# Opening of a two-layer decoder trunk: another order of the first loads and transposes, and a shorter run of warm-up matmuls

## The chip, the cores and the metric

The kernel runs on one core of a Trainium2 chip. The metric is the device time of one execution in microseconds (us), the median over several runs. The profile is one further execution on the same kind of chip.

## The reference

Two layers over 272 tokens (16 learned meta tokens in front of 256 tokens of x), model width 1024, float32. What matters here is the start: the first sub-layer norms the rows and multiplies them by the first weight matrix.

```python
h = jnp.concatenate([meta, x], axis=1)
for l in range(DEPTH):
    g = norm_g[l]
    h = h + 0.5 * rmsnorm(swiglu(rmsnorm(h, g[FFN1_PRE]), ffn_w_in[l, 0], ffn_w_out[l, 0]), g[FFN1_POST])
    ...   # pooling mixer, windowed attention, gated merge, second SwiGLU
return h[:, N_META:]
```

## The kernel before

Activations are kept transposed: `h` and `x_hi`/`x_lo` are eight tiles of 128 model columns by 272 tokens. Every float32 product is made of three matmuls on TensorE (function `products`, lines 451 to 453), with weights and activations split into a high and a low part: weights high by activations high, weights high by activations low, weights low by activations high. A "unit" is 256 output columns of a weight matrix (1024 KB, tile `raw`). SP loads units one after another into a ring of four slots; ScalarE makes `w_hi` from `raw`, VectorE makes `w_lo = raw - w_hi`. A whole unit is 2 x 8 x 3 = 48 matmuls of 272 columns.

The opening is written out by hand, in the order in which each engine's program lists it:

- **SP** (lines 344 to 356) loads the first half of x's columns, the second half, then the first half of unit 0 (line 366), its second half (line 356) and the further units. Each of the two halves of x and of unit 0 is 512 KB. The second half of x has a semaphore of its own, `second_half_in`.
- **ScalarE's queue** (lines 1037 to 1040) loads `norm_g` as 96 rows of 128 (the norms' rows), the meta tokens, and `pool_scale` as 8 more rows. These three and x's first half count on the one semaphore `inputs_in`.
- **TensorE** (lines 832 to 845) waits for the identity matrix, runs `WARM_FIRST` = 3 matmuls of the identity by itself, 512 columns each, whose result nobody reads, waits for all four transfers of `inputs_in`, transposes the 104 rows of norm gains and pool scales (`small`, bank 7), and then for each of the eight column blocks k transposes meta, first and second 128 tokens of x into bank k: a trio (lines 843, 844, 845). Ahead of k = 4 it waits for x's second half; ahead of k = 7 it waits until the rows in bank 7 have been read. Each trio raises `first_T`.
- **VectorE** copies the rows out (`g_all`, line 1501; `g_next`, the gains of the first norm, line 1503), and then, alternating with ScalarE, copies the trios into `h` (`first_h`, lines 1508 and 1047). ScalarE scales `h` into `x_hi` (line 1055), VectorE makes `x_lo` (line 1252), and between these unit 0 is split in four pieces of two column blocks each (`first_split`, line 1065 on ScalarE, line 1518 on VectorE).
- **TensorE** then runs the products of units 0 and 1 (`first_pair`): 12 matmuls for each piece of unit 0, each piece behind its own semaphore.

Of the kernel before, what the change touches and what calls it, by code (L numbers as in the profile page):

```python
# [33 lines left out]
P = 128  # L34
# [4 lines left out]
DEPTH = 2  # L39
# [9 lines left out]
KD = D // P  # L49
KF = FF // P  # L50
UW = 2 * P
# [35 lines left out]
NORMS = 6  # L87
# [56 lines left out]
def trunk(nc, x, meta_tokens, norm_g, ffn_w_in, ffn_w_out, w_in, pool_w_grp, pool_scale, w_pool_proj,  # L144
          sinks, w_attn_proj, w_o, geometry, out):
    with ExitStack() as ctx:
# [3 lines left out]
        def sem(name):  # L150
            return ctx.enter_context(nc.semaphore(name))


        raw = sb("raw", [P, RING, KD * UW])
# [21 lines left out]
        ident = sb("ident", [P, P])  # L176
        ones = sb("ones", [P, 1])
        g_all = sb("g_all", [P, DEPTH * NORMS * KD + DEPTH * GROUPS])
        g_cur = sb("g_cur", [P, NORMS * KD])
        half_g = sb("half_g", [P, KD])  # L180
        g_next = sb("g_next", [P, KD])
# [51 lines left out]
        n_rows = DEPTH * NORMS * KD + DEPTH * GROUPS  # L233
        first_rows = gates[0:n_rows, 12, 0:P]
# [6 lines left out]
        pT_bank, pTm_bank, o_bank, small = bank[4], bank[5], bank[6], bank[7]  # L241
        warm = o_bank
        S_SUM, S_BC = 0, 128


        inputs_in = sem("inputs_in")
        second_half_in = sem("second_half_in")
        geo_in = sem("geo_in")
        raw_landed = [sem(f"raw_landed{s}") for s in range(RING)]
# [8 lines left out]
        layer_consts = sem("layer_consts")  # L258
        first_T = sem("first_T")
        first_odd = sem("first_odd")  # L260
        first_raw = sem("first_raw")
# [3 lines left out]
        rows_read = sem("rows_read")  # L265
# [75 lines left out]
        @block.sync  # L341
        def _(sp):

            sp.dma_start(first_x[:, :, 0:D // 2], x[0, :, 0:D // 2].rearrange("(b p) d -> p b d", b=2)
                         ).then_inc(inputs_in, 16)
            sp.dma_start(first_x[:, :, D // 2:D], x[0, :, D // 2:D].rearrange("(b p) d -> p b d", b=2)
                         ).then_inc(second_half_in, 16)

# [4 lines left out]
            def load(u, src, dst=None):  # L353
                s = u % RING
                to = raw[:, s, 0:unit_k(u) * UW].rearrange("p (k c) -> p k c", c=UW) if dst is None else dst
                sp.dma_start(to, src).then_inc(raw_landed[s], 16)

            def ffn_loads(l, f):
                w1 = ffn_w_in[ds(l, 1), f].rearrange("o (k p) n -> p (o k) n", p=P)
                w2 = ffn_w_out[ds(l, 1), f].rearrange("o (k p) n -> p (o k) n", p=P)  # L360
                u0 = U_FFN_IN[f]
                for j in range(2):
                    slot_free(u0 + j, l)
                    if l == 0 and u0 + j == 0:
                        to = raw[:, 0, :].rearrange("p (k c) -> p k c", c=UW)
                        sp.dma_start(to[:, 0:KD // 2, :], w1[:, 0:KD // 2, 0:UW]).then_inc(first_raw, 16)
                        load(0, w1[:, KD // 2:KD, 0:UW], to[:, KD // 2:KD, :])
                    else:
                        load(u0 + j, w1[:, :, j * FF:j * FF + UW])
                with sp.Fori(0, N_IN - 5, 4) as i:  # L370
                    for j in range(4):
                        slot_free(u0 + 2 + j, l, i)
                        load(u0 + 2 + j, w1[:, :, ds(i * (UW // 2) + (UW * (1 + j // 2) + j % 2 * FF), UW)])
                u0 = U_FFN_OUT[f]
                if token_major(l, f):
                    for n in range(2):
                        for g, (k, nk) in enumerate(zip(END_K0, END_K)):
                            u = u0 + 6 * n + g
                            slot_free(u, l)
                            load(u, w2[:, k:k + nk, n * HALF_D:(n + 1) * HALF_D],  # L380
                                 raw[:, u % RING, 0:nk * HALF_D].rearrange("p (k c) -> p k c", c=HALF_D))
                    slot_free(u0 + N_END, l)
                    load(u0 + N_END, norm_g[l, NORMS - 1:NORMS, :].to_broadcast([P, D]), raw[:, (u0 + N_END) % RING, 0:D])
                    return
                with sp.Fori(0, N_OUT - 3, 4) as i:
                    for j in range(4):
                        slot_free(u0 + j, l, i)
                        load(u0 + j, w2[:, OUT_K0[j]:OUT_K0[j] + OUT_K[j], ds(i * (UW // 4), UW)])

            for l in range(DEPTH):  # L390
# [4 lines left out]
                for u in range(U_K, U_PP):  # L395
# [6 lines left out]
                    if U_Q <= u < U_POOL:  # L402

                        c = q0 + (8 * ((u - U_Q) // 2) + 2 * ((u - U_Q) % 2)) * DH
# [35 lines left out]
        def _(pe):  # L440
# [391 lines left out]
            pe.wait_ge(consts, 1)  # L832
            for _ in range(WARM_FIRST):
                pe.matmul(warm[:, :], ident[:, :], ident[:, :].unsqueeze(1).to_broadcast([P, 4, P]), start=True, stop=True)
            pe.wait_ge(inputs_in, 16 * 4)
            pe.transpose(small[:, 0:n_rows], first_rows, ident[0:n_rows, 0:n_rows]).then_inc(first_T, 1)
            for k in range(KD):
                if k == KD // 2:
                    pe.wait_ge(second_half_in, 16)
                if k == KD - 1:  # L840
                    pe.wait_ge(rows_read, 1)
                b = bank[k]
                pe.transpose(b[:, 0:META], first_meta[:, k * P:(k + 1) * P], ident[0:META, 0:META])
                pe.transpose(b[:, B1], first_x[:, 0, k * P:(k + 1) * P], ident[:, :])
                pe.transpose(b[:, B2], first_x[:, 1, k * P:(k + 1) * P], ident[:, :]).then_inc(first_T, 1)
# [15 lines left out]
        def _(act):  # L861
# [171 lines left out]
            def merge_hi(m, l):  # L1033
                act.wait_ge(merged, l * KD + m + 1)
                act.activation(x_hi[:, m, :], gates[:, m, :], ACT.Copy, scale=0.5).then_inc(xhi_ready, 1)

            act.dma_start(first_rows[0:DEPTH * NORMS * KD, :], norm_g.rearrange("l n (k p) -> (l n k) p", p=P)
                          ).then_inc(inputs_in, 16)
            act.dma_start(first_meta, meta_tokens).then_inc(inputs_in, 16)
            act.dma_start(first_rows[DEPTH * NORMS * KD:n_rows, :], pool_scale.rearrange("l (g p) -> (l g) p", p=P)  # L1040
                          ).then_inc(inputs_in, 16)
            act.preload_act_table(ACT.Silu)

            def first_h(k):

                act.wait_ge(first_T, k + 2)
                act.activation(h[:, k, :], bank[k][:, 0:T], ACT.Copy).then_inc(first_odd, 1)

            def first_operand(k):
# [19 lines left out]
            for piece in range(4):  # L1069
                k = 2 * piece  # L1070
# [12 lines left out]
            act.dma_start(sink_all[:, :], sinks.rearrange("(o l) h -> o (l h)", o=1).to_broadcast([P, DEPTH * HEADS])  # L1083
                          ).then_inc(geo_in, 16)
            split_hi(2, 0)
            act.wait_ge(inputs_in, 16 * 4)
            act.wait_ge(second_half_in, 16)
            scratch = y[:, :, :].rearrange("p k t -> p (k t)")
            for b, rows_of in enumerate((first_x[:, 0, :], first_x[:, 1, :], first_meta)):
# [75 lines left out]
        def _(dve):  # L1165
# [23 lines left out]

            def layer_columns(l):  # L1190
                dve.wait_ge(geo_in, 32)

                dve.wait_ge(xlo_ready, l * 4 * KD + KD)
                dve.wait_ge(h_ready, l * 3 * KD + KD)
                scales = DEPTH * NORMS * KD
                dve.tensor_copy(g_cur[:, :], g_all[:, ds(l * (NORMS * KD), NORMS * KD)])
                dve.tensor_copy(scale_cur[:, :], g_all[:, ds(l * GROUPS + scales, GROUPS)])
                for g in range(2):

                    dve.tensor_copy(sink_cur[:, 8 * g:8 * g + 8].rearrange("p (t s) -> p s t", s=2),  # L1200
                                           sink_all[:, ds(l * HEADS + 8 * g, 8)].rearrange("p (s t) -> p s t", s=2)
                                    ).then_inc(sinks_set, 1)

                dve.wait_ge(sinks_set, 2 * l + 2)
                dve.tensor_scalar(minus_sink[:, :], sink_cur[:, :], -1.0, None, ALU.mult)
                dve.tensor_scalar(half_g[:, :], g_all[:, ds(l * (NORMS * KD) + (NORMS - 1) * KD, KD)], 0.5, None, ALU.mult)

                dve.tensor_copy(g_next[:, :], g_all[:, ds(l * (NORMS * KD) + NORMS * KD, KD)]).then_inc(layer_consts, 1)
                dve.wait_ge(layer_consts, l + 2)
# [287 lines left out]
                                         ).then_inc(xlo_ready, 1)  # L1497


            dve.wait_ge(first_T, 1)  # L1500
            dve.tensor_copy(g_all[:, :], small[:, 0:n_rows]).then_inc(rows_read, 1)
            dve.wait_ge(rows_read, 1)
            dve.tensor_copy(g_next[:, :], g_all[:, 0:KD]).then_inc(layer_consts, 1)

            def first_h(k):

                dve.wait_ge(first_T, k + 2)
                dve.tensor_copy(h[:, k, :], bank[k][:, 0:T]).then_inc(h_ready, 2)

            def first_split(u, piece):  # L1510
# [8 lines left out]
                                  ).then_inc(lo_done if piece == pieces - 1 else first_lo, 1)  # L1519

            first_h(0)
            first_h(2)
            for piece in range(4):
                k = 2 * piece
                if piece == 0:
                    x_low(0, g_next, k)
                    first_split(0, 0)
                    x_low(0, g_next, k + 1)
                else:
                    x_low(0, g_next, k)  # L1530
                    x_low(0, g_next, k + 1)
                    first_split(0, piece)
                if piece < 2:
                    first_h(k + 4)
# [250 lines left out]
END_BANKS = ((4, 5), (0, 1))  # L1785
G_SLOT = (U_FFN_OUT[1] + N_END) % RING
Q_BANKS = ((4, 5), (0, 1), (2, 3), (0, 1))
WARM_FIRST = 3
WARM_RMS, WARM_X = 5, 5

META_STEP = 6
# [40 lines left out]
```

## Time and profile before

| | |
|---|---|
| Device time, median of 3 runs | 1208.03 us (1207.97 to 1208.48) |
| Device time of the profiled execution | 1207.88 us |
| Its span, first to last instruction | 1206.1 us |
| TensorE busy | 1193.3 us (99%) |
| VectorE, ScalarE, GpSimd busy | 708.4, 540.8, 448.4 us |
| Mean DMA rate | 164 GB/s |

The profile is of one execution. In the tables below PE is TensorE's matmul side and PEld its weight loads, DVE is VectorE, ACT ScalarE, POOL GpSimd, SP SyncE; a q behind a name (SPq, ACTq) is an engine's queue of issued transfers. A busy PE is not yet a PE at its peak, since matmuls are pipelined and their ends are modelled; it is the distance between starts that tells the pace. The device time of the profiled execution is 1.8 us longer than its span, for what lies around the instructions.

### The profile page before, as it was taken

The numbers are of one execution on the slowest core, as the hardware profiler recorded it, in microseconds if no ns is written. First come the engines' busy times: TensorE is split into PE (matmuls) and PEld (weight loads), VectorE is DVE, ScalarE is ACT, GpSimd is POOL, SyncE is SP. The second block draws the span as 40 slices with busy tenths as digits, with TensorE's granted clock in tenths as the row PEclk, the third lists the DMA queues.
The fourth block names the chain that finished last, engine by engine and source line by source line (L and its number), as shares of the span: only waits on it lengthen the run. The fifth ranks groups of instructions, "written<-read, shape, count | busy, mean of one in ns | idle before, by whom it ended". The sixth has DMA issues, their size and how long they took to land.

```text
span 1206.1 us, 23922 instructions
## 1 busy us (share of the span) xinstructions
PE 1193.3 (99%) x9352; PEld 1157.5 (96%) x9352; DVE 708.4 (59%) x1036; ACT 540.8 (45%) x763; POOL 448.4 (37%) x520
## 2 busy tenths in 40 slices
PE   9999999999999999999999999999999999999997
PEld 7999999999999999999999999999999999999986
DVE  6655544768666765544477554447776667755542
ACT  6433334536653453333344333344466545534441
POOL 0854500206312375542127554112064123865600
PEclk9999999999999999999999999999999999999999
DMA  9655357363355455535636553563734553655540
GB/s 315 201 174 165 123 184 226 102 210 108 100 134 189 136 176 174 174 122 172 215 120 198 181 171 117 185 200 110 226 124 106 166 185 105 210 189 176 180 169 35
DMA packets 197614, 197.59 MB, mean 164 GB/s; under 512 B 4136, under 2 KB 190736, under 8 KB 197536
## 3 DMA queue, kind: packets, MB, share of 16 engines
q1 hardware_dynamic: 197088, 196.10, 51.5%
q8 instruction: 56, 0.92, 0.3%
q10 hardware_dynamic: 448, 0.39, 0.1%
q14 instruction: 22, 0.18, 0.0%
HBM read 195.43 MB, written 1.05 MB: 163 GB/s over the span
## 4 chain that ended last, share of the span: by engine, by line
PE 93%; DVE 4%; issue 1%; POOL 1%; ACT 1%; DVEq 0%; POOLq 0%; ACTq 0%
PE bank L451 27%; PE bank L453 27%; PE bank L452 27%; PE bank L659 2%; PE bank L661 2%; PE bank L660 2%; DVE w_lo L1172 1%; PE bank L748 1%; PE bank L743 1%; PE bank L555 1%; DVE tmp L1261 1%; DVE h L1268 1%; PE bank L702 1%; DVE x_lo L1252 1%; PE bank L713 0%
## 5 line engine op out<-in xcount | busy, mean ns | idle before, releaser
L451 PE MATMUL bank<-x_hi,w_hi 128*128 128x272 f32 (+1 forms) x1988 | 575.0, 289 | 1.6 <-DVE up_r L1303 1.0
L453 PE MATMUL bank<-x_hi,w_lo 128*128 128x272 f32 (+1 forms) x1988 | 569.9, 287 | 0.0
L452 PE MATMUL bank<-x_lo,w_hi 128*128 128x272 f32 (+1 forms) x1988 | 568.3, 286 | 0.0
L870 ACT ACTIVATE w_hi<-raw 128x2048 fp32r<-128x2048 f32 (+2 forms) x210 | 352.6, 1686 | 436.6 <-PE bank L453 425.7
L1172 DVE TENSOR_TENSOR w_lo<-raw,w_hi 128x2048 fp32r<-128x2048 f32 (+3 forms) x208 | 423.8, 2045 | 164.4 <-ACT w_hi L870 159.3
L451 PEld LDWEIGHTS bank<-x_hi,w_hi 128*128 128x128 f32 x1988 | 374.6, 188 | 3.5 <-issue 1.5
L452 PEld LDWEIGHTS bank<-x_lo,w_hi 128*128 128x128 f32 x1988 | 374.4, 188 | 0.3
L453 PEld LDWEIGHTS bank<-x_hi,w_lo 128*128 128x128 f32 x1988 | 374.5, 188 | 0.0
L1718 POOL TENSOR_TENSOR hid_hi<-silu,up_r 128x272 f32 x88 | 140.4, 1595 | 177.1 <-DVE up_r L1303 157.1
L451 PE MATMUL bank<-hid_hi,w_hi 128*128 128x272 f32 x528 | 153.0, 290 | 0.0
L453 PE MATMUL bank<-hid_hi,w_lo 128*128 128x272 f32 x528 | 152.7, 289 | 0.0
L452 PE MATMUL bank<-hid_lo,w_hi 128*128 128x272 f32 x528 | 152.3, 288 | 0.0
L1303 DVE TENSOR_TENSOR up_r<-bank,r 128x272 f32<-128x272 f32 x88 | 38.4, 440 | 111.5 <-PE bank L453 103.7
L451 PEld LDWEIGHTS bank<-hid_hi,w_hi 128*128 128x128 f32 x528 | 99.6, 189 | 0.0
L452 PEld LDWEIGHTS bank<-hid_lo,w_hi 128*128 128x128 f32 x528 | 99.6, 189 | 0.0
L453 PEld LDWEIGHTS bank<-hid_hi,w_lo 128*128 128x128 f32 x528 | 99.3, 188 | 0.0
L1296 DVE TENSOR_TENSOR gate_r<-bank,r 128x272 f32<-128x272 f32 x88 | 38.0, 439 | 98.2 <-PE bank L453 98.1
L1723 POOL TENSOR_TENSOR hid_lo<-hid_f,hid_hi 128x272 f32 x88 | 87.9, 999 | 20.1 <-POOL hid_f L1720 20.1
L1702 POOL TENSOR_TENSOR acc<-acc,sq 128x272 f32<-128x272 f32 x50 | 41.8, 836 | 113.5 <-ACT sq L880 111.0
L1720 POOL TENSOR_TENSOR hid_f<-silu,up_r 128x272 f32<-128x272 f32 x88 | 77.6, 882 | 0.0
L1699 POOL TENSOR_TENSOR acc<-sq 128x272 f32<-128x272 f32 x10 | 11.7, 1166 | 153.5 <-ACT sq L880 153.5
L1754 POOL TENSOR_TENSOR acc<-s,stats 128x16 f32<-128x16 f32 x64 | 16.7, 261 | 89.5 <-DVE stats L1449 89.2
(204 smaller groups left out, 1277.9 us busy)
## 6 DMA issues: line engine op xcount, KB each, us to landing
raw<-in_ffn_w_in SPq DMA_DIRECT2D x87, 1024.0 KB, 5.1
raw<-in_w_in SPq DMA_DIRECT2D x24, 1024.0 KB, 5.6
raw<-in_ffn_w_out SPq DMA_DIRECT2D x24, 768.0 KB, 4.4
raw<-in_ffn_w_out SPq DMA_DIRECT2D x24, 640.0 KB, 4.0
raw<-in_ffn_w_out SPq DMA_DIRECT2D x10, 1024.0 KB, 5.1
raw<-in_w_in SPq DMA_DIRECT2D x16, 512.0 KB, 5.3
raw<-in_w_attn_proj SPq DMA_DIRECT2D x32, 256.0 KB, 4.2
raw<-in_w_o SPq DMA_DIRECT2D x8, 1024.0 KB, 5.4
```

The costliest lines, as they stand in the source:

```text
L451: pe.matmul(ps[:, t0:T], w[0], a_hi[:, t0:T], start=start, stop=False)
L452: pe.matmul(ps[:, t0:T], w[0], a_lo[:, t0:T], start=False, stop=False)
L453: return pe.matmul(ps[:, t0:T], w[1], a_hi[:, t0:T], start=False, stop=stop)
L659: pe.matmul(ps[:, :], hid_hi[:, k, cols], w[0], start=k == 0, stop=False)
L870: last = act.activation(hi, w, ACT.Copy)
L1172: last = dve.tensor_tensor(lo, w, hi.bitcast(F32), ALU.subtract)
L1296: dve.tensor_tensor(gate_r[:, j, :], bank[4 * (unit // 2 % 2) + j][:, 0:T], r[:, :], ALU.mult).then_inc(tile_read, 1)
L1303: dve.tensor_tensor(up_r[:, j, :], bank[2 + j][:, 0:T], r[:, :], ALU.mult).then_inc(tile_read, 1)
L1702: pool.tensor_tensor(acc[:, :], acc[:, :], sq[:, m % 2, :], ALU.add).then_inc(acc_done, 1)
L1718: pool.tensor_tensor(hid_hi[:, ds(i * 2 + j, 1), :].rearrange("p o t -> p (o t)"), silu[:, j, :], up_r[:, j, :], ALU.mult).then_inc(hid_hi ...
L1720: pool.tensor_tensor(hid_f[:, j, :], silu[:, j, :], up_r[:, j, :], ALU.mult).then_inc(hf_ready, 1)
L1723: pool.tensor_tensor(hid_lo[:, ds(i * 2 + j, 1), :].rearrange("p o t -> p (o t)"), hid_f[:, j, :], hid_hi[:, ds(i * 2 + j, 1), :].rearrang ...
```

## The change

SP now issues, in this order: the norms' rows (`norm_g`, which left ScalarE's queue), x's first half, the first half of unit 0, x's second half, the second half of unit 0. The norms' rows and the pool scales have a semaphore of their own (`rows_in`), so TensorE's first wait is for x's first half and the meta tokens alone. The transposed rows come ahead of k = 2 instead of ahead of k = 0. VectorE takes `g_next` straight from the bank between `first_h(0)` and `first_h(2)`, and `g_all` behind `first_h(2)`. The warm-up is one matmul of 512 columns and two of 256, for three of 512.

```diff
@@ block.sync
+            sp.dma_start(first_rows[0:DEPTH * NORMS * KD, :], norm_g.rearrange("l n (k p) -> (l n k) p", p=P)
+                         ).then_inc(rows_in, 16)
             sp.dma_start(first_x[:, :, 0:D // 2], x[0, :, 0:D // 2].rearrange("(b p) d -> p b d", b=2)
                          ).then_inc(inputs_in, 16)
+            first_w = ffn_w_in[0:1, 0].rearrange("o (k p) n -> p (o k) n", p=P)[:, :, 0:UW]
+            first_to = raw[:, 0, :].rearrange("p (k c) -> p k c", c=UW)
+            sp.dma_start(first_to[:, 0:KD // 2, :], first_w[:, 0:KD // 2, :]).then_inc(first_raw, 16)
             sp.dma_start(first_x[:, :, D // 2:D], x[0, :, D // 2:D].rearrange("(b p) d -> p b d", b=2)
                          ).then_inc(second_half_in, 16)
...
-                        to = raw[:, 0, :].rearrange("p (k c) -> p k c", c=UW)
-                        sp.dma_start(to[:, 0:KD // 2, :], w1[:, 0:KD // 2, 0:UW]).then_inc(first_raw, 16)
-                        load(0, w1[:, KD // 2:KD, 0:UW], to[:, KD // 2:KD, :])
+                        load(0, first_w[:, KD // 2:KD, :], first_to[:, KD // 2:KD, :])
@@ block.tensor
             for _ in range(WARM_FIRST):
                 pe.matmul(warm[:, :], ident[:, :], ident[:, :].unsqueeze(1).to_broadcast([P, 4, P]), start=True, stop=True)
-            pe.wait_ge(inputs_in, 16 * 4)
-            pe.transpose(small[:, 0:n_rows], first_rows, ident[0:n_rows, 0:n_rows]).then_inc(first_T, 1)
+            for _ in range(WARM_SHORT):
+                pe.matmul(warm[:, 0:2 * P], ident[:, :], ident[:, :].unsqueeze(1).to_broadcast([P, 2, P]), start=True, stop=True)
+            pe.wait_ge(inputs_in, 16 * 2)
             for k in range(KD):
+                if k == 2:
+                    pe.wait_ge(rows_in, 16 * 2)
+                    pe.transpose(small[:, 0:n_rows], first_rows, ident[0:n_rows, 0:n_rows]).then_inc(first_T, 1)
@@ block.scalar
-            act.dma_start(first_rows[0:DEPTH * NORMS * KD, :], norm_g.rearrange("l n (k p) -> (l n k) p", p=P)
-                          ).then_inc(inputs_in, 16)
...
             def first_h(k):
-                act.wait_ge(first_T, k + 2)
+                act.wait_ge(first_T, k + 1 if k < 2 else k + 2)
@@ block.vector
-            dve.wait_ge(first_T, 1)
-            dve.tensor_copy(g_all[:, :], small[:, 0:n_rows]).then_inc(rows_read, 1)
-            dve.wait_ge(rows_read, 1)
-            dve.tensor_copy(g_next[:, :], g_all[:, 0:KD]).then_inc(layer_consts, 1)
...
             first_h(0)
+            dve.wait_ge(first_T, 3)
+            dve.tensor_copy(g_next[:, :], small[:, 0:KD]).then_inc(layer_consts, 1)
             first_h(2)
+            dve.tensor_copy(g_all[:, :], small[:, 0:n_rows]).then_inc(rows_read, 1)
+            dve.wait_ge(layer_consts, 1)
...
-WARM_FIRST = 3
+WARM_FIRST, WARM_SHORT = 1, 2
```

SP's transfers at the start of the program, before:

```order
L344 DMA gates<-in_x 128x2x512
L346 DMA gates<-in_x 128x2x512
L366 DMA raw<-in_ffn_w_in 128x4x256 [waits lo_done]
L356 DMA raw<-in_ffn_w_in 128x4x256
L356 DMA raw<-in_ffn_w_in 128x8x256 [waits lo_done]
```

and with the change:

```order
L345 DMA gates<-in_norm_g 96x128
L347 DMA gates<-in_x 128x2x512
L351 DMA raw<-in_ffn_w_in 128x4x256
L352 DMA gates<-in_x 128x2x512
L362 DMA raw<-in_ffn_w_in 128x4x256 [waits lo_done]
L362 DMA raw<-in_ffn_w_in 128x8x256 [waits lo_done]
```

x's second half, second in SP's queue before, is now the fourth transfer and the third of 512 KB; `norm_g` stands ahead of all.

TensorE from the warm-up to the fifth trio (k = 4), before; the 128x104 row is the transpose of the norms' rows, a 128x16 row opens a trio:

```order
L834 MATMUL bank<-ident 128x512 [waits consts]
L834 MATMUL bank<-ident 128x512 x2
L836 MATMUL bank<-ident,gates 128x104 [waits inputs_in]
L843 MATMUL bank<-ident,gates 128x16
L844 MATMUL bank<-ident,gates 128x128
L845 MATMUL bank<-ident,gates 128x128
...
L843 MATMUL bank<-ident,gates 128x16 [waits second_half_in]
```

and with the change:

```order
L838 MATMUL bank<-ident 128x512 [waits consts]
L840 MATMUL bank<-ident 128x256 x2
L851 MATMUL bank<-ident,gates 128x16 [waits inputs_in]
L852 MATMUL bank<-ident,gates 128x128
L853 MATMUL bank<-ident,gates 128x128
...
L845 MATMUL bank<-ident,gates 128x104 [waits rows_in]
...
L851 MATMUL bank<-ident,gates 128x16 [waits second_half_in]
```

Two trios now stand ahead of the rows' transpose; the waits ahead of the fifth trio and of the eighth are where they were.

VectorE's first instructions, before:

```order
L1501 COPY g_all<-bank 128x104 [waits first_T]
L1503 COPY g_next<-g_all 128x8 [waits rows_read]
L1508 COPY h<-bank 128x272 [waits first_T] x2
L1252 SCALAR_TENSOR_TENSOR x_lo<-h,g_next,x_hi 128x272 [waits xhi_ready]
L1518 TENSOR_TENSOR w_lo<-raw,w_hi 128x512 [waits first_hi]
```

and with the change:

```order
L1510 COPY h<-bank 128x272 [waits first_T]
L1525 COPY g_next<-bank 128x8 [waits first_T]
L1510 COPY h<-bank 128x272 [waits first_T]
L1527 COPY g_all<-bank 128x104
L1259 SCALAR_TENSOR_TENSOR x_lo<-h,g_next,x_hi 128x272 [waits xhi_ready,layer_consts]
L1520 TENSOR_TENSOR w_lo<-raw,w_hi 128x512 [waits first_hi]
```

The copy `g_all` moved from the front to just ahead of the first `x_lo`.

## Rows read from the trace of the kernel before

**Rows 1.** Windows: us, PE busy (x), PEclk, DMA share, GB/s.
```profile
30.00:1200.00 1170.00, 1165.03 (x9178) 1.00 0.51 160
```

**Rows 2.** Chain of waits, opening: start us, us, what.
```profile
1.35 0.30 POOL ident L1691
1.70 5.45 PE bank L834 x6
7.15 0.26 PE bank L836
7.41 0.16 PE bank L843
...
11.28 0.26 PE bank L844
11.90 0.13 PE bank L453
```

**Rows 3.** Timeline, weight loads of TensorE: start us, us, what [idle before].
```profile
2.71 0.34 PEld L834 LDWEIGHTS bank<-ident 128*128 128x128 f32 x1 [0.52 <-issue]
...
4.42 0.34 PEld L834 LDWEIGHTS bank<-ident 128*128 128x128 f32 x1 [0.52 <-issue]
5.27 0.34 PEld L834 LDWEIGHTS bank<-ident 128*128 128x128 f32 x1 [0.52 <-issue]
7.10 0.14 PEld L836 LDWEIGHTS bank<-ident,gates 104*128 104x128 f32 x1 [1.49 <-DMA gates<-in_pool_scale]
```

**Rows 4.** Timeline, SP's issues of transfers.
```profile
0.75 0.45 SPq L344 DMA_DIRECT2D gates<-in_x  x1
1.27 0.45 SPq L346 DMA_DIRECT2D gates<-in_x  x1
1.77 0.46 SPq L366 DMA_DIRECT2D raw<-in_ffn_w_in  x1
```

**Rows 5.** Lines 346 and 366: from issue to landing.
```profile
L346 SPq DMA_DIRECT2D gates<-in_x x1: 445/445/445, 1.3 to 1.3; - x1
...
DMA to landing us min/median/max: 5.9/5.9/5.9
...
L366 SPq DMA_DIRECT2D raw<-in_ffn_w_in x1: 460/460/460, 1.8 to 1.8; - x1
...
DMA to landing us min/median/max: 6.9/6.9/6.9
```

**Rows 6.** Timeline, TensorE: fifth trio (k = 4), last transpose, first product.
```profile
9.46 0.23 PE L843 MATMUL bank<-ident,gates 16*128 16x16 f32 x1
...
9.99 0.23 PE L843 MATMUL bank<-ident,gates 16*128 16x16 f32 x1
...
11.40 0.37 PE L451 MATMUL bank<-x_hi,w_hi 128*128 128x272 f32 x1
```

**Rows 7.** Timeline, ScalarE and VectorE in the opening.
```profile
8.50 0.40 ACT L1047 ACTIVATE h<-bank 128x272 f32<-128x272 f32 x1 [4.82 <-PE bank L845]
8.80 0.51 ACT L1055 ACTIVATE x_hi<-h,g_next 128x272 fp32r<-128x272 f32 x1
...
7.45 0.27 DVE L1501 COPY g_all<-bank 128x104 f32<-128x104 f32 x1 [7.45 <-PE bank L836]
7.75 0.17 DVE L1503 COPY g_next<-g_all 128x8 f32<-128x8 f32 x1
...
9.46 0.49 DVE L1252 SCALAR_TENSOR_TENSOR x_lo<-h,g_next,x_hi 128x272 fp32r<-128x272 f32 x1
...
13.83 0.69 DVE L1518 TENSOR_TENSOR w_lo<-raw,w_hi 128x512 fp32r<-128x512 f32 x1
...
24.06 2.29 DVE L1172 TENSOR_TENSOR w_lo<-raw,w_hi 128x2048 fp32r<-128x2048 f32 x1 [1.52 <-ACT w_hi L870]
```

**Rows 8.** Timeline, weight loads around the third piece of unit 0.
```profile
14.12 0.19 PEld L452 LDWEIGHTS bank<-x_lo,w_hi 128*128 128x128 f32 x1
14.24 0.19 PEld L453 LDWEIGHTS bank<-x_hi,w_lo 128*128 128x128 f32 x1
14.57 0.19 PEld L451 LDWEIGHTS bank<-x_hi,w_hi 128*128 128x128 f32 x1
```

**Rows 9.** Weight loads of the identity, lines 834 and 565: ns min/median/max, first and last start us.
```profile
L834 PEld LDWEIGHTS bank<-ident x6: 287/337/337, 1.7 to 5.3; 128*128 128x128 f32 x6
...
L565 PEld LDWEIGHTS bank<-ident x60: 190/192/192, 214.4 to 824.8; 128*128 128x128 f32 x60
```

More of the change, by code:

```diff
@@ L246, in trunk @@
         inputs_in = sem("inputs_in")
+        rows_in = sem("rows_in")
         second_half_in = sem("second_half_in")
@@ L1035, in merge_hi @@
                 act.activation(x_hi[:, m, :], gates[:, m, :], ACT.Copy, scale=0.5).then_inc(xhi_ready, 1)
-            act.dma_start(first_rows[0:DEPTH * NORMS * KD, :], norm_g.rearrange("l n (k p) -> (l n k) p", p=P)
-                          ).then_inc(inputs_in, 16)
             act.dma_start(first_meta, meta_tokens).then_inc(inputs_in, 16)
             act.dma_start(first_rows[DEPTH * NORMS * KD:n_rows, :], pool_scale.rearrange("l (g p) -> (l g) p", p=P)
-                          ).then_inc(inputs_in, 16)
+                          ).then_inc(rows_in, 16)
             act.preload_act_table(ACT.Silu)
             def first_h(k):
-                act.wait_ge(first_T, k + 2)
+                act.wait_ge(first_T, k + 1 if k < 2 else k + 2)
                 act.activation(h[:, k, :], bank[k][:, 0:T], ACT.Copy).then_inc(first_odd, 1)
@@ L1085, in _ @@
             split_hi(2, 0)
-            act.wait_ge(inputs_in, 16 * 4)
+            act.wait_ge(inputs_in, 16 * 2)
             act.wait_ge(second_half_in, 16)
@@ L1191, in layer_columns @@
                 dve.wait_ge(geo_in, 32)
+                dve.wait_ge(rows_read, 1)
                 dve.wait_ge(xlo_ready, l * 4 * KD + KD)
@@ L1497, in merge_lo @@
                                          ).then_inc(xlo_ready, 1)
-            dve.wait_ge(first_T, 1)
-            dve.tensor_copy(g_all[:, :], small[:, 0:n_rows]).then_inc(rows_read, 1)
-            dve.wait_ge(rows_read, 1)
-            dve.tensor_copy(g_next[:, :], g_all[:, 0:KD]).then_inc(layer_consts, 1)
             def first_h(k):
-                dve.wait_ge(first_T, k + 2)
+                dve.wait_ge(first_T, k + 1 if k < 2 else k + 2)
                 dve.tensor_copy(h[:, k, :], bank[k][:, 0:T]).then_inc(h_ready, 2)
```

## The prediction

> **What bounds the kernel now.** I read the windows first, then the chain of waits, then the timeline of the opening engine by engine. From 30 to 1200 us TensorE is busy for 1165.0 of 1170 us [rows 1]. Behind the opening the kernel is one stream of matmuls, so a change of the opening is worth what it moves the start of that stream, unless something behind it is tied to absolute time. The chain of waits shows what sets that start [rows 2]: GpSimd makes the identity, TensorE runs the warm-up from 1.70 to 7.15, then the rows' transpose and the trios without a gap, and the first products follow. The first product starts at 11.40 [rows 6]. One gap remains in the first unit: weight loads follow each other by 0.12 or 0.13 us, except 14.24 to 14.57 [rows 8], a stall of 0.20, because the third piece of `w_lo` is ready only at 13.83 + 0.69 = 14.52 [rows 7].
>
> **Why the first transpose starts at 7.10.** The warm-up loads are 0.85 us apart (4.42 to 5.27), one for each pass of 512 columns, two passes to a float32 matmul [rows 3]. The first pass therefore starts at 2.71 - 0.85 = 1.86 and the six end at 1.86 + 6 x 0.85 = 6.97. The load for the rows' transpose starts at 7.10; the trace names the `pool_scale` transfer as what it waited for [rows 3]. So warm-up and inputs end within 0.13 us of each other and I can't tell which is last. Removing warm-up alone may then be worth nothing. The change does both: it shortens the warm-up and asks for fewer transfers first.
>
> **The change, part by part.**
>
> Warm-up: one matmul of 512 columns and two of 256 make 2 x 0.85 + 4 x 0.43 = 3.4 us, so it ends at 5.27 in place of 6.97: 1.7 us removed.
>
> First trio: it needs x's first half and meta. The trace has no landing for the first half. The second of SP's 512 KB transfers landed at 1.27 + 5.9 = 7.17 and the third at 1.77 + 6.9 = 8.67 [rows 4, 5], 1.50 apart; one step back gives 5.7 (an estimate). The issue now stands one place later, 0.52 us by the distance of SP's issues [rows 4], so 5.7 to 6.2. I take 6.2. Four trios at 9.99 - 9.46 = 0.53 [rows 6] and the rows' transpose at 0.26 [rows 2] make 2.4 us: k = 3 is done at 8.6.
>
> Fifth trio, the term that decides: it needs x's second half, before the second 512 KB of SP's queue and now the third. What was third landed at 8.67, and the same bytes stand ahead of it in both orders (`norm_g`, meta, `pool_scale`, two transfers of 512 KB). The ends: 8.67 if nothing is lost at the start, 9.2 if the whole queue slips by the 0.52 of one issue more. Less than that slips, as the small `norm_g` gives the engines something to move meanwhile: I take 8.80. With 0.05 from semaphore to start (the identity is done at 1.65, TensorE starts at 1.70 [rows 2]) the fifth trio starts at 8.85, and k = 3 is done by then. From fifth trio to first product took 11.40 - 9.46 = 1.94 [rows 6]. First product: 8.85 + 1.94 = 10.79, that is **0.61 earlier**. Moving x's second half back thus eats most of the 1.7 us of warm-up: TensorE waits there instead.
>
> The splits: ScalarE's chain was started by the second trio (`first_h(1)` at 8.50, `x_hi` at 8.80 [rows 7]). Now the second trio ends at 6.2 + 1.06 = 7.3, the rows are transposed by 7.5, `g_next` (0.17 [rows 7]) is there at 7.75, and the first half of unit 0, now second in the queue, has landed at 7.17 to 7.7. So ScalarE starts `x_hi` about 1.0 earlier. VectorE must take h for k = 2 (third trio done 8.1) and then the moved `g_all` (0.27 [rows 7]) ahead of the first `x_lo`: 8.1 + 0.4 + 0.3 = 8.8 against 9.46, 0.66 earlier. Between that `x_lo` and the third piece's end at 14.52 the timeline has no idle time of VectorE, so the third piece is ready at about 13.86. TensorE gets there at 10.79 + (14.37 - 11.40) = 13.76. Of the stall of 0.20 about 0.10 stays and **0.10 to 0.15 goes**.
>
> `g_all` behind `first_h(2)`: the eighth trio waits until bank 7 is read. That is at about 8.8, and the trio comes at 8.85 + 3 x 0.53 = 10.4. Cost nothing; a `g_all` 1.6 us later would begin to cost. One DMA moved from ScalarE's queue to SP's: ScalarE had nothing to do until 8.50 [rows 7], so nothing; its price on SP is the slip above. The wait for `rows_in`: `norm_g` is first of all and `pool_scale` second on ScalarE's queue, both small. They land ahead of the 7.3 at which TensorE asks. If `pool_scale` came with x's second half, ScalarE's chain would start at 9 and the gain would be gone.
>
> Later loads: the second half of unit 0 keeps its place as the fourth 512 KB. The `w_lo` of unit 3 is done at 24.06 + 2.29 = 26.35 [rows 7], while TensorE needs it three units of 48 x 0.125 = 6.0 us after 11.4, at 29.4: 3 us of slack, so an earlier stream doesn't run into its weights.
>
> Sum: 0.61 + 0.14 = 0.75 us less. For the profiled execution 1207.88 - 0.75 = 1207.1; the median of the runs stands 0.15 above it, so **1207.3 us**. A measurement of this kernel tells about 0.2% from no change, that is 2.4 us; the whole warm-up removed is less than that.
>
> **A rival on the other side: the clock rises later.** The granted clock reads 1.00 in every window, but the weight loads of the identity took 0.337 us in the warm-up and 0.192 from 214 us on, in the same form [rows 9], and the load at 7.10 took 0.14 [rows 3]. I read this as the lower level (1.2 GHz) up to about 7 us and the upper (2.4 GHz) from there, the warm-up having kept TensorE busy for 5.1 us before. The change gives it 3.4 us, a gap until x lands, then transposes with a gap before k = 4. The traces show that transposes behind the rise stayed quick; none shows a rise during transposes. If it does not come, the transposes cost between nothing and double. In the middle, times 1.5, the first four trios and the rows end at 6.2 + 3.6 = 9.8, the last four at 9.8 + 2.9 = 12.7. The 1.7 us of missing matmuls are then made up by products at half rate, which costs 0.85: 13.55 against 11.40, less the stall of 0.20, is 1.95 us more: **1210.0**. At the ends: if the transposes cost no more, 10.79 + 0.85 against 11.40, less 0.20, is +0.04; with all of them doubled and 5.1 us of products at half rate 6.2 + 4.8 + 3.9 + 2.55 = 17.45 less 11.40 and 0.20, +5.85. It decides when the clock is still low at 8.85. Against it: TensorE's work is nearly as dense as before up to 8 us. Chance 0.22.
>
> The Trainium skill (TensorE: Matmul & The Clock Gate, Part 4) says that the full clock doesn't engage for transpose-mode matmuls. By that rule the shorter warm-up is a loss, since from 5.3 us on only transposes could raise the clock; the rival above is what it would do here. The trace neither shows nor excludes it.
>
> **Rival: the queue slips whole.** x's second half lands at 9.2: the fifth trio starts 0.4 later, first product 11.19, and the chain of splits is then not late: 0.21 + 0.20 less, **1207.6**. For it: SP's issues are evenly spaced; against it: the bytes ahead are the same. Chance 0.13.
>
> **Rival: x lands sooner.** If the first half is there at 5.7 and the second at 8.1, the transposes run without a gap: first product 5.7 + 8 x 0.53 + 0.26 = 10.2, 1.2 earlier, and the stall goes too: **1206.6**. It needs the early transfers faster than any row shows. Chance 0.12.
>
> **How the numbers follow.** Forecast 1207.3 with 0.48, its own range 1207.0 to 1207.6; 0.05 stay for something not thought of. The range goes down to 1206.4 (x sooner) and up to 1209.8, which leaves out the worse half of the clock's rival and the unknown: some 0.15. Slower by over 0.2% (above 1210.4) only comes from that rival's upper end: 0.07. Faster by over 0.2% (below 1205.6) would need more than the whole warm-up: 0.01. Within 0.2%: 0.92.
>
> **What would show it.** In the profile after: warm-up loads ending near 4.9; the first trio at 5.5 to 6.2; a gap of TensorE ahead of the fifth trio, named as the transfer of x, until about 8.85; the first product at 10.8; the distance at the third piece 0.13 to 0.25; weight loads of the transposes 0.14 us long. Loads of 0.34 in the transposes, or products more than 0.13 apart behind the first, would show the clock's rival. No gap ahead of k = 4 would show that x lands sooner. The forecast is wrong if the first product starts before 10.3 or after 11.4, or if the move of the first product is not found in the total.

## The result, and the profile after

The changed kernel takes 1211.09 us (median of 21 runs, 1207.42 to 1211.70); the kernel before, run beside it, 1208.07 (21 runs). The medians are 3.02 us apart, 0.25%; the ratio of the two is 1.0019, 95% interval 1.0013 to 1.0025. **Slower, where 0.75 us less was forecast**, and above the range (1206.4 to 1209.8).

| | before | after |
|---|---|---|
| Device time of the profiled execution | 1207.88 us | 1211.70 us |
| Span | 1206.1 us | 1209.9 us |
| TensorE busy | 1193.3 us | 1196.2 us |
| First trio starts | 7.34 us | 6.57 us |
| First product starts [rows 6] | 11.40 us | 13.13 us |

The stream behind the opening is as dense as before [rows 1]: of 1170 us TensorE is busy for 1165.3 (window: us, PE busy, PEclk, DMA share, GB/s).

```profile
30.00:1200.00 1170.00, 1165.28 (x9187) 1.00 0.51 160
```

So the loss lies in the opening, or in a clock that this column of busy time does not see. TensorE in the timeline of the changed kernel (start us, us, engine, line, operation): the end of the warm-up, the first two trios, the fifth, the last transpose and the first products.

```profile
3.56 1.91 PE L840 MATMUL bank<-ident 128*128 128x256 f32 x4
6.57 0.28 PE L851 MATMUL bank<-ident,gates 16*128 16x16 f32 x1 [1.09 <-DMA gates<-in_x]
...
7.40 0.28 PE L851 MATMUL bank<-ident,gates 16*128 16x16 f32 x1
...
9.72 0.42 PE L853 MATMUL bank<-ident,gates 128*128 128x128 f32 x1
10.08 0.28 PE L851 MATMUL bank<-ident,gates 16*128 16x16 f32 x1
...
13.06 0.42 PE L853 MATMUL bank<-ident,gates 128*128 128x128 f32 x1
13.13 0.58 PE L455 MATMUL bank<-x_hi,w_hi 128*128 128x272 f32 x1
...
13.73 0.43 PE L457 MATMUL bank<-x_hi,w_lo 128*128 128x272 f32 x1
13.96 0.43 PE L455 MATMUL bank<-x_hi,w_hi 128*128 128x272 f32 x1
```

The trios are 0.83 us apart (6.57, 7.40) against 0.53 before [rows 6], the products 0.23 apart against 0.125. The weight loads show where that ends:

```profile
16.23 0.33 PEld L457 LDWEIGHTS bank<-x_hi,w_lo 128*128 128x128 f32 x1
16.45 0.33 PEld L455 LDWEIGHTS bank<-x_hi,w_hi 128*128 128x128 f32 x1
16.68 0.22 PEld L456 LDWEIGHTS bank<-x_lo,w_hi 128*128 128x128 f32 x1
16.84 0.19 PEld L457 LDWEIGHTS bank<-x_hi,w_lo 128*128 128x128 f32 x1
16.97 0.19 PEld L455 LDWEIGHTS bank<-x_hi,w_hi 128*128 128x128 f32 x1
```

Up to 16.7 us a load takes 0.33 us and the loads are 0.23 apart, from there 0.19 and 0.125. I read this as TensorE at its lower clock (1.2 GHz) through the whole opening and 3.6 us into the products, where before it was at the upper one (2.4 GHz) from about 7 us. The granted clock column does not help for this stretch: it reads 1.00 wherever the trace holds no earlier entry.

**The account.** First product later: 13.13 - 11.40 = 1.73. From 13.13 to 16.7 some sixteen products start 0.227 apart in place of 0.125: 1.6 more. The stall at the third piece of `w_lo` [rows 8] is gone, 0.2 less, as slow products give the splits time. Together 3.1; matched matmul by matmul, the two traces stand 3.12 apart from 30 to 300 us. Two steps follow, 0.35 at 618 us and 0.36 at 1008. Sum 3.83; the spans differ by 3.8. The second step is a dip of the clock:

```profile
1005.00:1010.00 5.00, 4.51 (x37) 1.00 0.16 40
1010.00:1013.40 3.40, 3.40 (x17) 0.50 1.07 369
1013.40:1200.00 186.60, 185.89 (x1333) 1.00 0.47 153
```

(Windows: us, PE busy, PEclk, DMA share, GB/s.) It falls at the norm ahead of the last feed-forward, where TensorE waits. This step goes with the execution and not with the change: e10 and e15 below are one kernel, and the clock dips in the one and not in the other (the same columns):

```profile
1005.75:1009.10 3.35, 3.35 (x18) 0.50 1.08 370
1005.75:1009.10 3.35, 2.98 (x24) 1.00 0.99 338
```

So of the 3.8 us between the two profiles 3.5 belong to the change. The chain of waits of the opening begins with SP's first transfer, then x's:

```profile
0.75 0.40 SPq L345
1.22 5.31 DMA gates<-in_x
6.57 0.28 PE bank L851
6.85 0.41 PE bank L852
```

Before, it began with the identity and the warm-up [rows 2]. The landings that answer to [rows 5], of x's first half (issued at 1.22) and its second half (issued at 2.19):

```profile
L347 SPq DMA_DIRECT2D gates<-in_x x1: 412/412/412, 1.2 to 1.2; - x1
...
DMA to landing us min/median/max: 5.3/5.3/5.3
...
L352 SPq DMA_DIRECT2D gates<-in_x x1: 507/507/507, 2.2 to 2.2; - x1
...
DMA to landing us min/median/max: 7.3/7.3/7.3
```

The first half was there at 6.5, the second at 9.5, both later than forecast (6.2 and 8.8). The second cost nothing here: the slow trios brought TensorE to the fifth only at 10.08, and the gap that the prediction puts ahead of it is not there.

### The profile page after: what moved, and what is told of

Same layout as the page of the kernel before. It is cut to its first block, busy times and chain, and to the rows that moved or that the text cites. A ratio compares the mean times of both kernels' runs of the same rounds, so it can differ in the third digit from the quotient of the medians.

```text
span 1209.9 us, 23925 instructions
## 1 busy us (share of the span) xinstructions
PE 1196.2 (99%) x9352; PEld 1161.5 (96%) x9352; DVE 708.0 (59%) x1036; ACT 541.0 (45%) x763; POOL 448.4 (37%) x520
## 4 chain that ended last, share of the span: by engine, by line
PE 94%; DVE 3%; issue 1%; POOL 0%; DMA 0%; ACT 0%; DVEq 0%; SPq 0%; POOLq 0%
PE bank L455 27%; PE bank L457 27%; PE bank L456 27%; PE bank L663 2%; PE bank L665 2%; PE bank L664 2%; PE bank L559 1%; PE bank L752 1%; PE bank L747 1%; DVE w_lo L1178 1%; DVE tmp L1268 1%; DVE h L1275 1%; PE bank L706 1%; DVE x_lo L1259 1%; PE bank L717 0%
## 5 line engine op out<-in xcount | busy, mean ns | idle before, releaser
L1760 POOL TENSOR_TENSOR acc<-s,stats 128x16 f32<-128x16 f32 x64 | 16.7, 261 | 89.5 <-DVE stats L1456 89.1
```

## The experiments

Each was timed beside the kernel before on the same chip. "Late" counts runs at 1210 us or above.

**e2, the short warm-up alone.**

```diff
 (kernel before)
-WARM_FIRST = 3
+WARM_FIRST, WARM_SHORT = 1, 2
...
+            for _ in range(WARM_SHORT):
+                pe.matmul(warm[:, 0:2 * P], ident[:, :], ident[:, :].unsqueeze(1).to_broadcast([P, 2, P]), start=True, stop=True)
```

> The kernel before with nothing but the short warm-up (one of 512, two of 256 columns). Theory clock: trios of 0.83 us and products 0.227 apart at first, 2 to 4 us slower in most runs. Theory loads: the loads are those of before, so no more than 0.3 us from before. A third outcome: the inputs land at 6.6, the trios then fill the time and the clock comes up some 3.4 us later, so 1 to 2 us slower.

Measured 1211.89 against 1208.50, ratio 1.0023 (1.0014 to 1.0032), 11 of 11 late. Its loads:

```profile
17.07 0.32 PEld L452 LDWEIGHTS bank<-x_lo,w_hi 128*128 128x128 f32 x1
17.30 0.21 PEld L453 LDWEIGHTS bank<-x_hi,w_lo 128*128 128x128 f32 x1
17.45 0.19 PEld L451 LDWEIGHTS bank<-x_hi,w_hi 128*128 128x128 f32 x1
```

The clock rose at 17.3, 3.1 us behind the first product (14.20), with all transfers in their old order. The warm-up alone makes the loss.

**e1, the change with the warm-up of before.**

```diff
 (changed kernel)
-WARM_FIRST, WARM_SHORT = 1, 2
+WARM_FIRST, WARM_SHORT = 3, 0
```

> The changed kernel with the warm-up of before (three matmuls of 512 columns). Theory clock: the loss of 3 us is the short warm-up; with the long one the granted clock is up by about 7 us as in the kernel before, the transposes take 0.53 us a trio, and the first product starts when x's second half has landed (9.48 in the changed kernel's trace) plus 0.05 and 1.94, at 11.5: within 0.3 us of the kernel before. Theory loads: the loss is the late landing of x (6.5 and 9.5), so the time stays about 3 us above before.

Measured 1208.44 against 1208.50, ratio 0.9995 (0.9986 to 1.0004), none of 11 late. The loss is gone.

```profile
6.63 0.23 PE L851 MATMUL bank<-ident,gates 16*128 16x16 f32 x1
...
7.16 0.23 PE L851 MATMUL bank<-ident,gates 16*128 16x16 f32 x1
...
10.78 0.37 PE L455 MATMUL bank<-x_hi,w_hi 128*128 128x272 f32 x1
```

Trios 0.53 apart, first product at 10.78, 0.62 earlier than before. x's second half landed at 8.7 here, the first in time for 6.63. The full warm-up took 5.00 us in this execution against 5.45 [rows 2], since the clock rose inside it; the start of the trios gains by that too, and it is not the work of the change. Behind the first unit the stream is 0.47 ahead of before; a step of 0.35 at 618 us and one of 0.37 at 1008 (the clock dips there in this execution too) take it back.

**e3, the norms' rows ahead of x, nothing else.**

```diff
 (kernel before; removed from ScalarE's queue, and ahead of x on SP's)
+            sp.dma_start(first_rows[0:DEPTH * NORMS * KD, :], norm_g.rearrange("l n (k p) -> (l n k) p", p=P)
+                         ).then_inc(inputs_in, 16)
```

> The kernel before with only the norms' rows moved to the head of SP's queue, all waits and the warm-up as before. If it is that transfer that made x's first half land at 6.5, it does so here (the rows' transpose then starts at 7.1 or later) and the first product moves by 0 to 0.5 us; if the mixing of the queues makes it, the landing of x's second half stays at 7.2 and nothing moves. Theory clock: 0 to 0.5 us, far from 3.

Measured 1207.88 against 1208.50, ratio 0.9987 (0.9978 to 0.9997); ten of 11 between 1207.42 and 1208.19, one at 1438.83. The four inputs were in by 6.4, not 7.1, and the first product started at 10.70. In the profile the gain was lost at once (span 1206.1, as before), because the first half of unit 0, third of the 512 KB transfers, landed at 9.3 and ScalarE waited for it:

```profile
8.07 0.51 ACT L1055 ACTIVATE x_hi<-h,g_next 128x272 fp32r<-128x272 f32 x1
9.29 0.63 ACT L1065 ACTIVATE w_hi<-raw 128x512 fp32r<-128x512 f32 x1 [0.70 <-DMA raw<-in_ffn_w_in]
```

and TensorE behind it, 0.64 and 0.22 ahead of the second and the third piece:

```profile
12.89 0.19 PEld L453 LDWEIGHTS bank<-x_hi,w_hi 128*128 128x128 f32 x1 [0.64 <-DVE w_lo L1518]
...
14.66 0.19 PEld L453 LDWEIGHTS bank<-x_hi,w_hi 128*128 128x128 f32 x1 [0.22 <-DVE w_lo L1518]
```

The median is lower than the profile explains. Part of that is that none of the ten was late, where 9 of the 33 runs beside it were: the others of those have their median at 1208.25, 0.4 above e3's.

**e4, e1 with x's second half ahead of the first half of unit 0.**

```diff
 (e1; block.sync)
-            sp.dma_start(first_to[:, 0:KD // 2, :], first_w[:, 0:KD // 2, :]).then_inc(first_raw, 16)
             sp.dma_start(first_x[:, :, D // 2:D], x[0, :, D // 2:D].rearrange("(b p) d -> p b d", b=2)
                          ).then_inc(second_half_in, 16)
+            sp.dma_start(first_to[:, 0:KD // 2, :], first_w[:, 0:KD // 2, :]).then_inc(first_raw, 16)
```

> The changed kernel with the warm-up of before and x's second half ahead of the first half of unit 0. Theory clock: the clock is up by 7 us, no gap ahead of k = 4; the rows' transpose no longer stands ahead of the first trio, so the second trio ends 0.25 us earlier, the first product starts at 7.10 + 0.25 + 8 x 0.53 = 11.35 or so: between 0 and 0.3 us faster than before. Theory loads: the same as e1 less what the second half waited, so slower than before as long as the rows stand ahead of x.

Measured 1208.34, ratio 0.9995 (0.9986 to 1.0004), none of 11 late. First product at 10.72, then the same waits as in e3 (ScalarE 0.69, TensorE 0.58 and 0.22): behind the first unit it is level with before. e1, with weights ahead of x, is 0.47 ahead there, without the long waits. That the new order of transfers is worth this half microsecond is not shown: the medians of e1 and e4 are 1208.44 and 1208.34, and e10 and e15, both with the new order, are 0.63 and 0.10 ahead at the same place.

**e8, e1 with the norms' rows back at the head of ScalarE's queue.**

```diff
 (e1)
-            sp.dma_start(first_rows[0:DEPTH * NORMS * KD, :], norm_g.rearrange("l n (k p) -> (l n k) p", p=P)
+            act.dma_start(first_rows[0:DEPTH * NORMS * KD, :], norm_g.rearrange("l n (k p) -> (l n k) p", p=P)
```

> e1 (the change's order, warm-up of before) with the norms' rows back at the head of ScalarE's queue, so that x's first half is first on SP's. If the rows ahead of x delay it, x's first half lands about 0.5 us earlier than in e1 and the second half at 8.2 to 8.7; the first product then starts at 10.3 to 10.7 and the time is 0 to 0.5 us below e1. If the warm-up's end sets the first trio, nothing changes against e1.

Measured 1208.33 against 1208.53, ratio 0.9994 (0.9986 to 1.0003), none of 12 late. x's second half landed at 9.2, not 8.7, and the stream was level with before. The landings of one order differ by half a microsecond and more between executions (8.7, 9.0 and 8.9 in e1, e10, e15; 9.5 in the changed kernel), so one profile each does not settle which queue is better. Inconclusive.

**e7, a warm-up of 4.3 us** (as e2, with two matmuls of 512 columns and one of 256).

```diff
 (kernel before)
-WARM_FIRST = 3
+WARM_FIRST, WARM_SHORT = 2, 1
```

> The kernel before with a warm-up of two matmuls of 512 columns and one of 256, 4.3 us in all, between the 3.4 of e2 and the 5.1 of before. If whether the clock rises depends on where the start of the program falls, this length should give both outcomes: some runs near 1208, some 3 us above, the median in either place. If there is a sharp length, all runs are alike.

Measured 1211.49, ratio 1.0017 (1.0008 to 1.0025), 12 of 12 late: as bad as 3.4 us. The clock rose at 17.7.

**e5 and e6, what the warm-up is made of.**

```diff
 (kernel before; e5, with WARM_FIRST = 20)
-                pe.matmul(warm[:, :], ident[:, :], ident[:, :].unsqueeze(1).to_broadcast([P, 4, P]), start=True, stop=True)
+                pe.transpose(warm[:, 0:P], ident[:, :], ident[:, :])
 (e6, with WARM_FIRST = 12)
+                pe.matmul(warm[:, 0:P], ident[:, :], ident[:, :], start=True, stop=True)
```

> The kernel before with its warm-up made of 20 transposes of the identity (128 columns each, 0.26 us apart at the lower clock, 5.2 us in all) in place of three matmuls of 512 columns (5.1 us). Theory kind (transposes do not bring the clock up): the clock rises only 3 to 4 us after the first product, as in e2, and the time is 3 to 4 us above before. Theory length (any 5 us of TensorE work do): as before, within 0.3 us.

> The counterpart: 12 plain matmuls of the identity, 128 columns each, about 5.1 us in all. Both theories: the clock rises by 7 us and the time is that of before within 0.3 us. If this too is 3 us slower, it is the width of the matmuls and not their kind.

e6: 1208.93, ratio 1.0002 (0.9992 to 1.0011), 3 of 10 late. Narrow matmuls do as well as wide ones. e5: 1211.43, ratio 1.0017 (1.0008 to 1.0027), 10 of 10 late. The time seems to speak for "kind", but e5 does not have the length that was meant: its transposes started 0.21 us apart, not 0.26, so twenty of them make 4.3 us in place of 5.1, as short as e7's warm-up, and e7 was late in all runs with plain matmuls. The time doesn't separate kind from length. The trace speaks against "kind":

```profile
1.70 4.53 PE L834 MATMUL bank<-ident 128*128 128x128 f32 x20 [1.70 <-POOL ident L1691]
...
8.72 0.23 PE L843 MATMUL bank<-ident,gates 16*128 16x16 f32 x1
...
9.25 0.23 PE L843 MATMUL bank<-ident,gates 16*128 16x16 f32 x1
...
10.50 0.28 PE L843 MATMUL bank<-ident,gates 16*128 16x16 f32 x1
```

and its windows (us, PE busy, PEclk, DMA share, GB/s):

```profile
6.65:10.00 3.35, 2.58 (x15) 1.00 1.10 348
10.10:16.80 6.70, 6.70 (x29) 0.50 1.10 348
16.90:20.00 3.10, 3.10 (x27) 1.00 1.10 344
```

The trios stood 0.53 apart at first: transposes alone had brought the clock up. Then it fell at 10.06, during the trios, 2.6 us behind the 1.2 us of idle time ahead of them, and came back only at 16.9. What this execution lost it lost by falling. A gap alone doesn't do it: e6 had 1.26 us idle ahead of the rows' transpose and kept the clock.

**e14, the change once more; e15 beside it; e13.**

> The changed kernel itself, on the same chip and in the same rounds as e15: 2 to 3.5 us above before, with most runs at 1210.2 or above.

Measured 1211.05 against 1208.23, ratio 1.0017 (1.0008 to 1.0026), 11 of 11 late. This execution loses by another way, 1.9 us in the opening and 2.7 in all:

```profile
7.73 0.27 PE L853 MATMUL bank<-ident,gates 128*128 128x128 f32 x1
9.06 0.28 PE L851 MATMUL bank<-ident,gates 16*128 16x16 f32 x1 [1.06 <-DMA gates<-in_x]
...
9.89 0.28 PE L851 MATMUL bank<-ident,gates 16*128 16x16 f32 x1
```

```profile
5.00:8.40 3.40, 2.58 (x15) 1.00 1.04 375
8.45:15.20 6.75, 6.14 (x25) 0.50 1.10 350
15.30:20.00 4.70, 4.70 (x39) 1.00 1.10 345
```

The clock rose at 5.0, fell at 8.4 in the gap ahead of the fifth trio, where TensorE waits for x's second half, and rose again at 15.2, 3.1 us behind the first product. The new order of transfers makes that gap (x's second half landed at 9.0), and the short warm-up had raised the clock here all the same. So the change has two ways to lose: the clock doesn't rise in time, or it rises and falls again.

```diff
 (e13: the changed kernel, behind each trio)
+                if k < KD - 2:
+                    pe.matmul(warm[:, 0:2 * P], ident[:, :], ident[:, :].unsqueeze(1).to_broadcast([P, 2, P]), start=True, stop=True)
```

> The changed kernel with its short warm-up, and behind each of the first six trios one plain matmul of the identity, 256 columns (0.85 us at the lower clock, 0.43 at the upper). Read by the clock, not by the time. Theory trios too thin: the transposes between 6.6 and 13.1 did not bring the clock up because they leave TensorE's array idle between them; with the filler it comes up before the first product, by about 10 us. Rival (only the stretch before the data counts, whatever comes behind): it rises again 3 to 4 us behind the first product. The time is 1 to 3.5 us above before by the first, 6 or more by the rival.

e13 measured 1210.65, ratio 1.0017 (1.0007 to 1.0027), four of its 8 runs at 1209.1 to 1209.8 and four at 1211.5 to 1212.9. In its profile the clock had risen at 5.5, ahead of any filler, and stayed up, past 1.0 us of idle time ahead of the first trio. So it doesn't say whether filler can bring the clock up. Inconclusive.

**e9 and e10, the step at 618 us.** Kernels with the change's code show VectorE idle ahead of `x_hi` at the norm into layer 1, here e1:

```profile
616.61 0.50 DVE L1268 SCALAR_TENSOR_TENSOR tmp<-y,g_cur,bank 128x272 f32<-128x272 f32 x1 [0.28 <-PE bank L580]
617.58 0.50 DVE L1282 SCALAR_TENSOR_TENSOR x_hi<-tmp,gain,r 128x272 fp32r<-128x272 f32 x1 [0.47 <-DVE tmp L1268]
```

```diff
 (e9: kernel before, layer_columns)
                 dve.wait_ge(geo_in, 32)
+                dve.wait_ge(rows_read, 1)
 (e10: e1, layer_columns)
                 dve.wait_ge(geo_in, 32)
-                dve.wait_ge(rows_read, 1)
```

> The kernel before with one more instruction on VectorE in layer_columns, the wait for rows_read that the change adds and that is long fulfilled when it is reached. In all four traces of kernels with the change's code the matmul stream loses 0.35 us at 618 us, where VectorE stands 0.47 us ahead of the x_hi of layer 1's first norm; in none of the five with the code of before. Theory place of the code: this kernel shows the 0.35 us at 618 too. Rival (it comes from the order of the opening): nothing at 618.

> e1 without the added wait in layer_columns. Theory place of the code: the step of 0.35 us at 618 is gone, the opening's gain of 0.5 us stays, the median is 0.3 to 0.4 below e1 and 0.4 to 0.8 below before: faster than both kernels if it holds. Rival: the step stays and the time is that of e1.

e9: 1208.37 against 1208.81, ratio 1.0001 (0.9992 to 1.0011), 3 of 10 late, no step at 618. Its opening settles a question of the prediction, whether warm-up or inputs end last in the kernel before: the warm-up was over at 6.2, the clock having risen early, and TensorE still waited for the inputs, as it did in e2, e5, e6 and e7 (until 7.23 to 7.44):

```profile
7.05 0.31 PE L836 MATMUL bank<-ident,gates 104*128 104x104 f32 x1 [0.82 <-DMA gates<-in_pool_scale]
```

e10: **1207.90** against 1208.81, ratio 0.9989 (0.9980 to 0.9998), none of 11 late, and the step is gone:

```profile
616.46 0.50 DVE L1267 SCALAR_TENSOR_TENSOR tmp<-y,g_cur,bank 128x272 f32<-128x272 f32 x1 [0.28 <-PE bank L580]
617.07 0.50 DVE L1281 SCALAR_TENSOR_TENSOR x_hi<-tmp,gain,r 128x272 fp32r<-128x272 f32 x1
```

The step stands in all six traces of kernels with the change's code and this wait (the change, e1, e4, e8, e13, e14) and in none of the others. The added wait costs 0.35 us in the changed program and nothing in the old one. That it is the place of the code was only half borne out; the cause stays open.

> e10 once more: 0.5 to 1 us below before, 3 us below the change, and no run at 1210 or above. If the late rise of the clock in some runs of before is a matter of chance alone and not of its idle time ahead of the rows' transpose, this kernel shows it too in about one run of four.

e15 is e10 beside the change: 1207.77 against 1208.23 before, ratio 0.9995 (0.9986 to 1.0004), 3.3 below the change's 1211.05, none of 11 late. Against the runs of before that were not late (medians 1208.32 and 1208.19) e10 and e15 are both 0.4 lower; the rest of e10's 0.9 is late runs beside it.

**e11 and e12, a longer warm-up** (four matmuls of 512 columns).

```diff
 (e11: e10)
-WARM_FIRST, WARM_SHORT = 3, 0
+WARM_FIRST, WARM_SHORT = 4, 0
 (e12: kernel before)
-WARM_FIRST = 3
+WARM_FIRST = 4
```

> e10 with a fourth warm-up matmul of 512 columns: 6.8 us at the lower clock, less where the clock rises inside it. If warm-up past the landing of x only delays the first trio, it is 0 to 1 us slower than e10 (the fourth matmul takes 0.85 us at the upper clock, 1.7 at the lower). If the length makes a late rise of the clock rarer, no run is above 1210.

> The kernel before with a fourth warm-up matmul. In its own runs about one in four lies at 1210.6 to 1211.3. If those are runs in which the clock rose late, they are gone here, the others are 0.9 to 1.7 us slower (TensorE gets to the rows' transpose at 7.9 to 8.7 in place of 7.1), so all lie near 1209 to 1209.8. If the share at 1210.6 and above stays, it has another cause.

e11: 1209.08, ratio 0.9999 (0.9990 to 1.0008), none of 11 late, but 1.2 above e10. In its profile the clock fell at 11.5, just as the products began, 2.0 us behind a gap of 0.45 ahead of the fifth trio, and came back at 14.9:

```profile
9.53 0.23 PE L851 MATMUL bank<-ident,gates 16*128 16x16 f32 x1 [0.45 <-DMA gates<-in_x]
...
11.55:14.90 3.35, 3.35 (x17) 0.50 1.10 348
```

(Timeline, then a window: us, PE busy, PEclk, DMA share, GB/s.) So a longer warm-up doesn't by itself keep the clock up either. e12: 1208.95 against 1208.81, ratio 0.9995 (0.9986 to 1.0004), none of 11 late, where the kernel before had 11 of 33; its first product is 1.16 later (12.56), which is the price of the added matmul.

No late run of the kernel before was profiled, but the mean granted clock of each run was taken. All 36 late ones are at 0.995 to 0.997. The 71 at 0.998 or above are all below 1209 us but for one at 2980. A late first rise does not lower this figure (the changed kernel's profiled run, at its lower clock up to 16.7 us, has 0.998), a fall does (e14's has 0.995). That speaks for late runs of before in which the clock had risen and fallen, as in e14 and e5; where it fell is not shown.

## Why the prediction was wrong

- **The step that failed** is "Warm-up: 1.7 us removed". I took the length of the warm-up as a cost, put its effect on the clock at nothing in the sum (trios 0.53 apart from 6.2, products 0.125 apart from 10.79), and left it to a rival with 0.22. e2 shows the effect decides: the same edit alone gives 3.4 us more, where the profiled trios are 0.83 apart and the products 0.23 apart up to 17.3. The right reading of the identity's weight loads [rows 9] was in the text and should have carried the forecast: a warm-up that ends within 0.13 us of the inputs costs almost nothing to keep, and e9's wait shows that in this order the inputs are the later of the two.
- **The rival had the right mechanism and was too small.** It took transposes at 1.5 times; they are at 0.83 / 0.53 = 1.57. It took products at half rate for 1.7 us, "the missing matmuls"; they ran so for 3.6 us, 1.6 lost in place of 0.85. With the first trio at 6.57 in place of 6.2 the total was 3.1 in the opening, not 1.95. It has only a clock that rises late; that it can rise and fall again in the gap ahead of the fifth trio (e14) stands in no rival. The range, cut at 1209.8, left out even that rival's own value of 1210.0.
- **The rule of the Trainium skill** (TensorE: Matmul & The Clock Gate, Part 4), that the full clock doesn't engage for transposes, pointed to the right side. e5 contradicts it as a rule: 20 transposes in a row brought the clock up. What these traces show instead is that a stream of trios behind a short warm-up didn't bring it up (after, e2, e7) or didn't hold it (e5, e14). It held it in e13, and in e6 and e9 behind idle times of 1.26 and 0.82 us, so what decides is open.
- **The fifth trio.** With the clock up (e1, e10, e15) x's second half landed at 8.7, 9.0 and 8.9 against 8.80: about right. That e1's first product started at 10.78 against 10.79 is luck. TensorE did not wait for x there; its trios ran without a gap from 6.63, when the full warm-up was over, to the fifth at 8.84. The forecast's wait is in e10 (0.36 us, first product 10.99). In the change's own executions the landing was 9.5 and 9.0: the end I had put at 9.2 was too low.
- **The stall at the third piece** was to lose 0.10 to 0.15. In e1 it stayed (0.22), and the opening, 0.62 ahead at the first product, kept 0.47.
- **The added wait.** The change also puts a wait for `rows_read` into VectorE's `layer_columns`, which neither the diff ahead of the prediction nor its sum has. I had put it at nothing without a reason; in this program it costs 0.35 us at 618 (e10 against e1).
- **"Within 0.2%: 0.92"** went with the same step; the change is at the edge of it, 0.25% by the medians and 0.19% by the ratio.

## What to carry to other kernels

Before shortening a warm-up, find what it hides behind (here the landing of the inputs, 0.13 us later) and what clock the work behind it gets; in e7 0.85 us less of idle matmuls cost 3 us. Then change one thing. Two versions with the old warm-up were the fastest here: the new order of transfers without one needless wait (1207.90 and 1207.77 against 1208.81 and 1208.23), and the norms' rows ahead of x and nothing else (1207.88 against 1208.50). Compare many runs, and like with like: the runs of a kernel whose clock hangs on the opening fall into levels two to three us apart, and a median moves with the share of late ones.

## What was not expected of the hardware

- With warm-ups of 3.4 and 4.3 us 53 of 55 runs were late (the change, e14, e2, e7), while with 5.1 us and the first trio ahead of the rows' transpose none of 56 was (e1, e4, e8, e10, e15). The kernel before, with 5.1 us, was late in 36 of 127 runs beside the experiments (the one at 2980 us left out). Whether the length of the warm-up decides or that it reaches up to the first real work, no run separates.
- Once up, the clock fell in the opening in three executions: inside a gap of 1.06 us (e14), and 2.6 and 2.0 us behind gaps of 1.19 and 0.45 us (e5, e11). It stayed down for 6.8 us in e14 and e5 and for 3.4 in e11. In e6, e9 and e13 gaps of 0.8 to 1.3 us did nothing.
- With a wait that is long fulfilled VectorE stood idle for 0.47 us, at a place behind it, in one program and not in another, with the same instructions around it.
